# Residual rows stored unscaled in column blocks, and nine expert weight pieces fetched ahead of the mixture

## The reference

```python
x = x + mod_lat[:, 2] * merge_heads(o_m, o_n, ..., w_out[l])      # x1: the residual stream
h2 = modulate(rms_norm(x, g_norm2[l]), mod_lat[:, 3], mod_lat[:, 4])
x = x + mod_lat[:, 5] * expert_choice_ffn(h2, w_router[l], w_gate[l], w_up[l], w_down[l])

def expert_choice_ffn(h, w_router, w_gate, w_up, w_down):
    aff = softmax(einsum('btd,de->bte', h, w_router))
    g, idx = lax.top_k(aff.transpose(0, 2, 1), cap)               # 64 tokens for each of 16 experts
    xs = h[idx]
    y = einsum('becf,efd->becd', silu(xs @ w_gate) * (xs @ w_up), w_down) * g
    return zeros.at[idx].add(y)
```

## Time and profile before

| | |
|---|---|
| median of 3 runs | 2093.07 us (2092.68 to 2094.48) |
| the profiled execution | 2088.43 us |
| its span, first to last instruction | 2086.5 us |
| TensorE busy | 1938.2 us, 93% of the span |
| VectorE, ScalarE, GpSimd busy | 832.6, 427.1, 174.4 us |
| DMA | 602.78 MB, of which the expert weights are 403 MB |
| granted TensorE clock, mean | 0.987 |

### The profile page before, as it was taken

One profiled execution on the slowest core, in us unless ns is written; L12 is line 12 of the kernel. 1 busy time (PEld: TensorE's weight loads), 2 busy tenths in 40 slices (PEclk: granted clock), 3 DMA queues, 4 the chain that ended last, 5 costly groups with the idle time before them and its releaser, 6 DMA issues.

```text
span 2086.5 us, 25707 instructions
## 1 busy us (share of the span) xinstructions
PE 1938.2 (93%) x10114; PEld 1231.2 (59%) x10114; DVE 832.6 (40%) x1723; ACT 427.1 (20%) x1141; POOL 174.4 (8%) x402
## 2 busy tenths in 40 slices
PE   4899999999999999989996999998989999898988
PEld 2578788878877777768885533433435353443433
DVE  5557877773245555534444131221303021121303
ACT  4223223122145555532222000000000000000000
POOL 0003112011133322200000000000000000000000
PEclk9999999999999999999997999999999999999999
DMA  9937888783122111132228999999999999999998
GB/s 403 421 141 270 325 294 291 270 282 138 46 102 86 45 44 44 43 134 81 81 81 353 395 419 429 427 427 428 427 428 427 428 427 427 428 428 427 426 428 355
DMA packets 77079, 602.78 MB, mean 289 GB/s; under 512 B 7568, under 2 KB 25232, under 8 KB 33568
## 3 DMA queue, kind: packets, MB, share of 16 engines
q1 hardware_dynamic: 64224, 591.11, 70.0%
q10 hardware_dynamic: 12592, 8.98, 1.3%
q0 software_dynamic: 144, 1.05, 0.1%
HBM read 584.32 MB, written 16.79 MB: 288 GB/s over the span
## 4 chain that ended last, share of the span: by engine, by line
PE 50%; DMA 11%; DVE 2%; ACT 2%; issue 1%; POOL 0%; DVEq 0%; ACTq 0%
DMA arena<-in_w_gate_up 10%; PE SM L1115 7%; PE TM L1115 7%; PE SM L1145 6%; PE TM L1145 5%; PE TR L1064 3%; PE MJ L1064 2%; PE TM L919 1%; PE SM L885 1%; PE SN L1102 1%; DMA wor<-in_w_out 1%; PE MJ L817 1%; PE MJ L821 1%; PE SM L890 1%; PE SM L960 1%
## 5 line engine op out<-in xcount | busy, mean ns | idle before, releaser
L1115 PE MATMUL SM<-arena 128*64 128x512 f32 x1024 | 245.0, 598 | 47.2 <-DMA arena<-in_w_gate_up 46.7
L1115 PE MATMUL TM<-arena 128*64 128x512 f32 x1024 | 242.7, 592 | 0.0
L1683 DVE SCALAR_TENSOR_TENSOR arena<-arena,csil 128x512 f32<-128x512 f32 x240 | 180.3, 751 | 46.7 <-DMA arena<-in_w_mod 38.3
L1115 PEld LDWEIGHTS SM<-arena 128*64 128x64 f32 x1024 | 71.0, 136 | 191.4 <-issue 190.5
L1115 PEld LDWEIGHTS TM<-arena 128*64 128x64 f32 x1024 | 78.6, 137 | 141.1 <-issue 141.1
L1145 PE MATMUL SM<-arena 128*64 128x512 f32 x512 | 117.8, 609 | 1.5 <-DVE arena L2011 1.5
L1145 PE MATMUL TM<-arena 128*64 128x512 f32 x512 | 116.9, 599 | 0.0
L1203 ACT ACTIVATE wh<-wr 128x2048 fp32r<-128x2048 f32 (+1 forms) x32 | 58.7, 1835 | 192.4 <-PE TN L720 148.8
L1931 DVE TENSOR_TENSOR arena<-cst,rope_t 128x512 f32<-128x512 f32 x8 | 5.5, 692 | 230.3 <-PE MJ L1088 230.3
L718 PE MATMUL SM<-wh,h_hi 128*128 128x512 f32 (+1 forms) x224 | 89.2, 398 | 7.8 <-DVE h_lo L1631 7.8
L1413 ACT CAST y_hi<-arena 128x512 fp32r<-128x512 f32 x32 | 19.8, 619 | 367.7 <-DVE arena L1967 367.7
(11 more groups left out here) (327 smaller groups left out, 3488.1 us busy)
## 6 DMA issues: line engine op xcount, KB each, us to landing
arena<-in_w_gate_up SPq DMA_DIRECT2D x128, 2048.0 KB, 16.3
arena<-in_w_down SPq DMA_DIRECT2D x64, 2048.0 KB, 25.5
arena<-in_w_mod SPq DMA_DIRECT2D x96, 1024.0 KB, 5.5
wr<-in_w_na SPq DMA_DIRECT2D x24, 1024.0 KB, 7.0
wor<-in_w_out SPq DMA_DIRECT2D x8, 2048.0 KB, 7.9
xT<-in_tokens_t SPq DMA_DIRECT2D x4, 1536.0 KB, 12.6
arena<-in_w_qkv SPq DMA_DIRECT2D x8, 640.0 KB, 5.4
wr<-in_w_qa SPq DMA_DIRECT2D x4, 1024.0 KB, 11.9
```

What stands on the lines that cost most here:

```text
L1115: mm = pe.matmul(GU[b][64 * e:64 * e + CAP, :], xsT[:, k, 64 * e:64 * e + CAP], w[:, 2 * (b // 2) + e, (b % 2) * NB:(b % 2 + 1) * NB], sta ...
L1683: ve.scalar_tensor_tensor(acc, row, c, acc, ALU.mult, ALU.add).then_inc(mod_step, 1)
```

## The change

- SP stores x1's column blocks 0 to 2 to x1_d, unscaled, four stores of 256 KB each, behind the loads of the w_out half-blocks 3, 5 and 7. Block 3 is stored by ScalarE's own queue, tile by tile, behind the routing step of that tile.
- ScalarE scales x1 in place only when all 16 stores have landed.
- Column 1 of `token_no` is overwritten with e_rs, so that `find_rows` yields each fetched row's e_rs beside its index; VectorE copies it out (`rows_rs`), and ScalarE scales the 128 fetched rows once they have landed. TensorE's transposes for pair 1 wait for that.
- A ninth weight piece (8) is fetched ahead, into 128 K to 144 K, when the projection and the routing are done with that place. `member_1` moves. Pieces 4 to 7 wait for y_full in place of y_free.
- The gate2 broadcast is issued just before piece 15, after use 10.

With `PRE` = 9, pieces 9 to 14 follow the uses 1 to 6, and piece n from 15 on follows use n - 5.

```diff
-PRE = 8
+PRE = 9
-SLOT_AT = [4, 5, 0, 2, 6, 7, 1, 3]
+SLOT_AT = [4, 5, 0, 2, 6, 7, 1, 3, 8]
-        member_1 = arena.take(136 * K, LT, P)
+        member_1 = arena.take(152 * K, LT, P)
+        rows_rs = st[:, 25:26]
@@ SP
             for p in range(2, 2 * MODB):
                 sp.wait_ge(y_full, LT * (p - 1))
                 load_w_out(p)
+                if p >= 3 and p % 2:
+                    nb = p // 2 - 1
+                    cols = slice(nb * NB, (nb + 1) * NB)
+                    sp.wait_ge(x1_add, LT * (2 * nb + 2))
+                    for tile in range(LT):
+                        sp.dma_start(x1_d[tile * P:(tile + 1) * P, cols], x1[:, tile, cols]).then_inc(x1_out, 16)
...
-            sp.wait_ge(y_free, LT * 2 * MODB)
-            for n in range(4, PRE):
+            sp.wait_ge(y_full, LT * 2 * MODB)
+            for n in range(4, PRE - 1):
                 moe_load(n)
-            sp.dma_start(gate2_b[:], modrow_d[1:2, :].partition_broadcast(P)).then_inc(gate2_in, 16)
-            for tile in range(LT):
-                sp.wait_ge(x1_scaled, tile + 1)
-                sp.dma_start(x1_d[tile * P:(tile + 1) * P, :], x1[:, tile, :]).then_inc(x1_out, 16)
+            sp.wait_ge(x1_add, LT * 2 * MODB)
+            sp.wait_ge(lg_part, LT * MODB)
+            moe_load(PRE - 1)
             for n in range(PRE, PAIRS * PIECES):
                 before = n - PRE if n < PRE + RING else n - RING
                 sp.wait_ge(moe_used, before + 1)
+                if before == PRE:
+                    sp.dma_start(gate2_b[:], modrow_d[1:2, :].partition_broadcast(P)).then_inc(gate2_in, 16)
                 moe_load(n)
@@ TensorE
                     if q == 0:
-                        pe.wait_ge(rows_in, 16)
+                        pe.wait_ge(rows_set, 1)
...
                 pe.wait_ge(member_set, 2)
+                pe.wait_ge(idx_set, 1)
...
                 if pair == 0:
-                    pe.wait_ge(idx_set, 1)
+                    pe.wait_ge(idx_set, 2)
@@ ScalarE
+                if (kind, a) == ("route", MODB - 1):
+                    sc.wait_ge(x1_add, LT * (2 * MODB - 1) + tile + 1)
+                    sc.dma_start(x1_d[tile * P:(tile + 1) * P, D - NB:D], x1[:, tile, D - NB:D]).then_inc(x1_out, 16)
+            sc.wait_ge(x1_out, 16 * LT * MODB)
             for tile in range(LT):
                 sc.wait_ge(e_rsd, 2 * tile + 1)
                 sc.activation(x1[:, tile, :], x1[:, tile, :], ACT.Copy, scale=e_rs[:, tile:tile + 1]).then_inc(x1_scaled, 1)
...
+                if pair == 0:
+                    sc.wait_ge(rows_in, 16)
+                    sc.activation(rows_1, rows_1, ACT.Copy, scale=rows_rs).then_inc(rows_set, 1)
@@ GpSimd
-            po.wait_ge(idx_set, 1)
-            po.wait_ge(x1_out, 16 * LT)
+            po.wait_ge(idx_set, 2)
+            po.wait_ge(x1_out, 16 * LT * MODB)
@@ VectorE
             def members_ahead():
+                ve.wait_ge(e_rsd, 2 * LT)
+                ve.tensor_copy(token_no[:, :, 1], e_rs).then_inc(idx_set, 1)
...
                 ve.wait_ge(idx_full, 1)
+                ve.tensor_copy(rows_rs, SN[:, 1:2])
                 ve.tensor_copy(idx_1, SN[:, 0:1]).then_inc(idx_set, 1)
```

More of the change, by code:

```diff
@@ L500, in build_layer @@
             sem(n) for n in ("silu_done", "act_done", "at2_full", "at2_free", "y_done"))
-        idx_full, idx_set, x1_out, rows_in = sem("idx_full"), sem("idx_set"), sem("x1_out"), sem("rows_in")
+        idx_full, idx_set, x1_out, rows_in, rows_set = (
+            sem(n) for n in ("idx_full", "idx_set", "x1_out", "rows_in", "rows_set"))
         y_high, y_low, mt_full, mt_set, add_full, acc_done = (
```

## The result

| | before | changed |
|---|---|---|
| median | 2092.57 us (20 runs, 2089.20 to 2095.93) | 2096.79 us (20 runs, 2090.65 to 2105.17) |
| ratio | 1 | 1.0024, 95% interval 1.0016 to 1.0031 |
| profiled execution, span | 2088.43, 2086.5 us | 2094.86, 2093.1 us |

The changed kernel is slower by 4.2 us in the medians, 5.0 by the ratio. It lies in the predicted range (2089.0 to 2098.5) and on the side that I had given 0.14: the forecast was no change, 2093.1. Its runs also spread over 14.5 us where those of the kernel before spread over 6.7. The profiled execution of the kernel before is shorter than each of its 20 runs above, that of the changed kernel 1.9 us shorter than its median.

A forecast was written before the change was run, and what follows sets the result against it. The prediction took the expert phase's weight stream, plus a fixed tail, to bound the kernel. Its terms summed to +0.0 us (between -0.1 and about +2.5), so it forecast 2093.1 us, range 2089.0 to 2098.5.

The forecast's parts named there:

- the side that I had given 0.14: Whole kernel: the changed kernel comes out slower, chance 0.14, against 0.77 for the same and 0.09 for faster.
- parts 1, 2, 6: Weight stream: ninth piece ahead, +0.02 us; residual stores and gate2 moved, 0; pieces 4 to 7 waiting for y_full, 0.
- Rival C: Weight stream: the ninth piece counts in full, 2088.2 us, or 2090.6 with gate2's 2.5 us charged; chance 0.09.
- part 4: ScalarE's scaling of x1 waits for all sixteen stores; last landing at 1133.5, 3.6 us to spare, cost 0.
- the 9.0 us row: Profile row behind part 4's assumed landing: 256 KB store, same queue, beside 2 MB of weights; 9.0 us, median 2.1.
- Rival B: Last store on ScalarE's queue lands behind all pieces in flight; gathers start 8.7 us late, 2101.8 us; chance 0.14.
- part 5: VectorE copies e_rs and ScalarE scales the fetched rows, 1.9 us, in an idle stretch of 74 us: cost 0.
- part 3: Column-block stores from SP behind out-projection weight loads and from ScalarE: cost 0, at most 1.3 us of queue.

The follow-up runs named there:

- e5: Changed kernel with a second broadcast of the same 1024 KB issued right behind gate2, ahead of piece 15: 2099.57 us, 1.0033 of the kernel before.
- e3: Changed kernel with eight pieces fetched ahead again and gate2 loaded where piece 8 was: 2096.52 us, 1.0023 of the kernel before.
- e10: e9 with e1's wait, gate2 issued at use 9 and pair 0's fourth gather one piece later: 2087.56 us, 0.9977 of the kernel before.
- e11: Kernel before with the w_out split behind tile 1's residual and pair 0's fourth gather before piece 11: 2088.72 us, 0.9981 of the kernel before.
- e4: Changed kernel with block 3's four stores issued by SP behind pieces 4 to 7 instead of by ScalarE's queue: 2109.90 us, 1.0074 of the kernel before.
- e2: Kernel before with only the twelve block stores added, into a tensor nobody reads: 2097.75 us, 1.0025 of the kernel before.
- e9: Changed kernel with the w_out split moved from behind tile 0's residual to behind tile 1's: 2089.89 us, 0.9984 of the kernel before.
- e7: e2 with each store 32 columns wide instead of 512, a sixteenth of the bytes: 2091.28 us, 0.9993 of the kernel before.
- e1: Changed kernel with SP issuing the twelve block stores only when the w_out load ahead has landed: 2092.75 us, 0.9995 of the kernel before.

## Why the prediction was right or wrong

**Right: the stream (parts 1, 2, 6).** The ninth piece, the stores' bytes taken out of the stream and gate2 put into it were to come to +0.02 us. From the second gather to piece 16's issue it is 1208.53 - 1164.97 = 43.56 us in the changed kernel and 1201.25 - 1157.69 = 43.56 in the kernel before, and from that gather to the end of the last gate/up wait 874.50 against 874.35; such a close match of the second pair is partly luck, given its scatter (e5), but the ends of the first gate/up wait match as well (e3). e3 tested the account from one side, e5 from the other, e10 and e11 drew a gain from it. Rival C is out in full, and very unlikely with gate2 charged to it. The times forecast on the clock of the trace missed, as the whole phase moved: piece 16 is issued at 1208.53 and not within 0.5 us of 1201.25, the first gather starts at 1151.06 and not at 1144.8, the last gate/up wait ends at 2039.5 and not near 2032. Two readings were careless without touching the sum: 426 to 429 GB/s holds in 15 of the 40 slices, not in the last 46% of them, and a free gate2 would have made the difference 0, not -0.02 us, as piece 16 waits for its own issue in both kernels.

**Right: ScalarE's wait (part 4).** Slack 3.6 us forecast, 3.7 found, partly by luck: the landing took 1.2 us longer than assumed, and the issue came 21.7 us ahead of the gather where 20.3 were reckoned. The sentence that a store waits behind one piece at most is not borne out: 10.2 us is 8.1 above the 2.1 of an undisturbed store, and a piece takes 4.91; the 9.0 us row was 6.9 above it. Rival B's price, 8.7 us, was of the right size where e4 made it true, 10.5 by the ratios and 13.1 by the medians.

**Right: rows scaled when fetched (part 5).** ScalarE's 2.00 us lie in a long idle stretch, as said.

**Wrong: part 3, "being queued behind the load and 20 us ahead of the next, they delay none", and so "Cost 0".** The stores are indeed done long before the next load, and I took the queue's order to protect the load ahead, too. It doesn't: stores issued 1.5 us behind the load make it land later, while it is still moving. I had even put a price on the issue (1.3 us of queue, 1.8 in the trace) and none on the transfer, and I looked at the 52 us slices, which average over a load and a rest, instead of at the 8 us in which the load runs. Nor did I ask who waits for that landing: the earlier trace rows were read from 1298.7 on only, while three w_out loads stood in the same chain ahead. What the term measured instead of 0: 0.75 us of landing on average, 2.8 us of stalls in the profiled execution, and with a half-clock stretch 4.5; in medians 4.2 us (the whole change) and 4.7 us (e2). It was paid through the order of work on VectorE, the logits behind the split behind the load, as e9 shows.

The chances were therefore too sure of no change. Of the rivals none was this one; the one that ended on the slow side, B, had another mechanism.

## What to carry to other kernels

Ahead of moving a transfer to a "quiet" time, look at the microseconds right behind its issue, not at a slice's mean, and find the load that is in flight then and the first engine that waits for it. In this stream, what was freed ahead of a hole was worth nothing; find the last hole in the binding stream and what ends it, here a slot that returns only at use 11. When a stall grows, ask in which order the waiting engine holds its work: one tile's delay of the split was worth 3 us in the kernel before, while the change, with its cost removed, is worth less than can be measured here.

## What the runs showed of the hardware

Stores disturbed a load that was issued ahead of them on the same queue. Windows of the kernel before, then of the changed one, in the last microseconds of half-block 3's load (last columns: DMA share, GB/s); the changed kernel's load was issued 1.74 us later, so its second line compares with the first of the kernel before:

```profile
974.00:976.00 2.00, 2.00 (x12) 1.64 (x11) 0.04 (x1) 0.00 (x0) 0.00 (x0) 1.00 0.90 385
976.00:978.00 2.00, 2.00 (x16) 1.84 (x15) 1.41 (x3) 1.10 (x2) 0.00 (x0) 1.00 0.00 0
```

```profile
974.00:976.00 2.00, 2.00 (x11) 1.65 (x10) 0.00 (x0) 0.00 (x0) 0.00 (x0) 1.00 1.06 401
976.00:978.00 2.00, 2.00 (x14) 1.68 (x12) 0.31 (x1) 0.00 (x0) 0.00 (x0) 1.00 1.04 287
```

In the changed kernel the engines are busy at a share of 1.04 but move 287 GB/s, load and stores together, against 385 at 0.90: the packets take longer on average; whether those of the load or of the stores, this view does not tell. e7 says that the stores' bytes matter and their number little. The Trainium skill (DMA: Bandwidth & Descriptors, Queues, rings and completion order) says that within one ring descriptors are consumed in order but carry no barrier; that agrees with two transfers of one queue being under way together. What they share that makes the packets longer is open.

Small stalls can cost more than themselves. In the profiled execution the granted clock fell to 0.50 behind a stall of 1.42 us; it fell at the same kind of place behind 1.25 us in e1, 1.38 in e2, 1.36 in e3, 1.73 in e5, and 1.90 and 1.71 in e4. It did not behind 1.32 and 1.18 us in the same changed kernel, 1.29 in e7, 1.44 in e3 and 1.49 in e2, so the length of the stall alone does not decide it, and what does is open. In the 20 runs of the changed kernel the slowest, 2105.17 us, had a mean granted clock of 0.981 and the second fastest, 2090.96, one of 0.988, and over all 20 a longer run goes with a lower clock (correlation -0.81). That such stretches make its spread fits this. It was not tried by itself, e2 and e3 with the same stores spread over only 5 and 6 us in eight runs each, the kernel before over 8.8 and 9.0 us in other sets of 23 and 35 runs. How many of the 6.9 to 8.4 us between the changed kernel and e9 such stretches make is not settled.
